# Rotation by copies, one turn for eight conditioning blocks, and tile sums added before the norm's matmul

## What is computed

```
mod_lat, mod_ctx = silu(c) @ w_ada + b_ada, silu(c_ctx) @ w_ada + b_ada     # 6144 columns each
sh_m, sc_m, gt_m, sh_f, sc_f, gt_f = split(mod_lat, 6)                      # shift, scale, gate
u = x * (1 + sc_m) + sh_m ;  u_ctx = ctx * (1 + csc_m) + csh_m
q, k, v, g, glu, gates = split(u @ w_in + b_in)
t1, t2 = split(q, 2) per head of 128 ;  rot = concat(-t2, t1)
q = q * cos + rot * sin                                                     # the same for k
o = bidirectional retention of q, k, v (8 heads), with states from u_ctx
z = depthwise convolution (31 taps) of za * sigmoid(zb)
z = silu((z - mean(z)) * rsqrt(mean((z - mean)^2) + eps) * g + b)           # over the 1024 channels
mix = (ga * (ret @ w_ret_out) + gb * (z @ w_conv_out + b_conv)) @ w_mix_out + b
h = LN(ALPHA * x + gt_m * mix) ;  mixture of 32 experts on h * (1 + sc_f) + sh_f ;  LN
```

## Time and profile before

| | us |
|---|---|
| median of 3 runs | 1581.92 |
| lowest, highest | 1580.75, 1583.12 |
| the profiled execution | 1583.5 |
| its span in the profile | 1581.6 |
| TensorE busy in the span | 1494.8 (95%) |
| VectorE busy | 492.7 (31%) |
| ScalarE busy | 214.1 (14%) |
| TensorE's mean granted clock, share of full speed | 0.986 |

### The profile page before, as it was taken

One profiled execution on the slowest core, in us unless ns is written; L12 is line 12 of the kernel. 1 busy time (PEld: TensorE's weight loads), 2 busy tenths in 40 slices (PEclk: granted clock), 3 DMA queues, 4 the chain that ended last, 5 costly groups with the idle time before them and its releaser, 6 DMA issues.

```text
span 1581.6 us, 19250 instructions
## 1 busy us (share of the span) xinstructions
PE 1494.8 (95%) x8272; PEld 948.0 (60%) x8272; DVE 492.7 (31%) x1107; ACT 214.1 (14%) x423; POOL 18.6 (1%) x39
## 2 busy tenths in 40 slices
PE   4999999999999989999999999898999899999997
PEld 2876644575588878555554444444788786555543
DVE  1546696453100125222221121123223224122222
ACT  1100100121111102311111001002022012110111
POOL 0000000000000001000000000000010000000000
PEclk8999999999999989999999999999999999999999
DMA  9522313364443464799999999999463646899996
GB/s 391 216 106 109 118 60 120 138 241 166 166 159 112 156 266 182 271 419 426 428 426 427 427 426 427 427 427 386 108 224 113 240 153 257 367 428 426 426 397 263
DMA packets 33896, 436.00 MB, mean 276 GB/s; under 512 B 4096, under 2 KB 5640, under 8 KB 7576
## 3 DMA queue, kind: packets, MB, share of 16 engines
q1 hardware_dynamic: 29520, 423.38, 66.1%
q10 hardware_dynamic: 2472, 6.41, 1.5%
q0 software_dynamic: 1824, 5.05, 0.9%
HBM read 432.19 MB, written 2.62 MB: 275 GB/s over the span
## 4 chain that ended last, share of the span: by engine, by line
PE 80%; DMA 16%; DVE 3%; ACT 1%; issue 0%; POOL 0%; SPq 0%; ACTq 0%; DVEq 0%; POOLq 0%
PE PP L751 26%; PE PP L1009 16%; PE PP L764 13%; PE PP L1024 8%; DMA RA<-in_w_moe 6%; PE MB L993 5%; DMA KQ<-in_w_moe 4%; DMA ring<-in_w_moe 4%; PE PP L985 1%; DMA ring<-in_w_glu 1%; PE PP L740 1%; PE MB L850 1%; PE MB L832 1%; DMA ring<-in_w_ada 1%; PE MB L853 1%; PE PP L1017 1%
## 5 line engine op out<-in xcount | busy, mean ns | idle before, releaser
L751 PE MATMUL PP<-uT,ring 128*128 128x256 f32 x1024 | 226.4, 384 | 3.9 <-DMA ring<-in_w_glu 3.9
L751 PEld LDWEIGHTS PP<-uT,ring 128*128 128x128 f32 x1024 | 196.8, 193 | 32.6 <-issue 5.4
L1009 PE MATMUL PP<-ring,const 128*64 128x256 f32 x1312 | 151.9, 386 | 13.2 <-DMA ring<-in_w_moe 8.0
L1009 PEld LDWEIGHTS PP<-ring,const 128*64 128x64 f32 x1312 | 96.8, 139 | 73.9 <-issue 17.1
L764 PE MATMUL PP<-ring,uT 128*128 128x512 f32 x288 | 125.1, 593 | 0.0
L1269 DVE SCALAR_TENSOR_TENSOR ZC<-ZC,vec 128x256 f32<-128x256 f32 x240 | 116.4, 485 | 8.6
L993 PE MATMUL MB<-V 64*128 64x512 f32 x400 | 112.4, 640 | 1.7 <-DVE V L1657 0.9
L1634 DVE TENSOR_SCALAR V<-V 128x1 f32<-128x1 f32 x50 | 7.7, 154 | 312.1 <-PE PP L1009 312.1
L764 PEld LDWEIGHTS PP<-ring,uT 128*128 128x128 f32 x288 | 54.4, 190 | 67.6 <-issue 67.6
L1649 DVE SCALAR_TENSOR_TENSOR V<-V 128x256 f32<-128x256 f32 x100 | 48.5, 485 | 120.5 <-PE MB L993 93.8
L764 PE MATMUL PP<-ring,RA 128*128 128x512 f32 x192 | 83.4, 592 | 0.0
(11 more groups left out here) (376 smaller groups left out, 1485.2 us busy)
## 6 DMA issues: line engine op xcount, KB each, us to landing
ring<-in_w_moe SPq DMA_DIRECT2D x61, 2048.0 KB, 18.1
RA<-in_w_moe SPq DMA_DIRECT2D x25, 2048.0 KB, 17.0
ZC<-in_w_moe SPq DMA_DIRECT2D x25, 2048.0 KB, 16.7
KQ<-in_w_moe SPq DMA_DIRECT2D x20, 2048.0 KB, 19.2
Vc<-in_w_moe SPq DMA_DIRECT2D x19, 2048.0 KB, 17.7
ring<-in_w_ada SPq DMA_DIRECT2D x12, 2048.0 KB, 8.4
ring<-in_w_gates SPq DMA_DIRECT2D x7, 2048.0 KB, 7.9
ring<-in_w_v SPq DMA_DIRECT2D x5, 2048.0 KB, 7.7
```

The costliest lines, as they stand in the source:

```text
L751: ins = pe.matmul(out[:, c, :], W[:, k * width + at:k * width + at + P], X[:, k, :], start=k == 0, stop=k == K - 1)
L1009: ins = pe.matmul(bank[q][SLOTS * g:SLOTS * (g + 1), 0:L], x[:, k, :], W[:, k * 512 + g * 256:k * 512 + (g + 1) * 256], start=k == 0, stop ...
```

## The change

Rotation: `rotate`, its matrix and its eight matmuls go. After `raw_copy`, ScalarE copies partitions 64 to 127 of `raw` to 0 to 63 of a buffer `swapped` (the memory of `Ph`), and 0 to 63 to 64 to 127; the sign goes into the sine table. The PSUM pair is released before these copies.

Conditioning: for blocks 4 to 11, the window of `sT` that serves as the left side is moved by one column per block, so that block 4 + i puts its result into row i of each group of 32 and zero into the others. All eight accumulate in one PSUM pair, which is copied once and turned once with an eight-column selection. The later jobs' pairs are counted anew. `late_modulation` follows the statistics of the last head.

Norm: VectorE adds the eight tiles of `conv` (behind the last convolution step), and later of the squares (behind `ret(0)`), into `rs`; one matmul for each sum remains.

```diff
-                     ("rot", 128), ("pick", 2), ...
+                     ("pick", 9), ...
-                    dense += 1
+                    dense += src != "ada" or b < 4 or b == 11
-        sT = sb("sT", [P, DT, 32])
+        sT = sb("sT", [P, DT, 40])
+        swapped = Ph
-            nc.scalar.activation(sT[:, :, 0:2], cin[:, :, :], ACT.Silu).then_inc(silu_c, 1)
+            nc.scalar.activation(sT[:, :, 0:9:8], cin[:, :, :], ACT.Silu).then_inc(silu_c, 1)
...
-                ins.then_inc(pair_free[j["pair"]], 1)
+                say(act, ins, pair_free[j["pair"]], j["use"] + 1)
+                nc.scalar.activation(swapped[0:64], raw[64:128], ACT.Copy)
+                nc.scalar.activation(swapped[64:128], raw[0:64], ACT.Copy).then_inc(raw_swapped, 1)
...
-                        ins = pe.matmul(out[at:at + 32, 0:2, :]..., sT[:, k, :],
-                                        W[:, k * 512:(k + 1) * 512], start=k < 4, stop=k >= 4, tile_position=(0, at))
+                        at, late = 32 * (k % 4), j["b"] - 4
+                        x = sT[:, k, 0:32] if late < 0 else sT[:, k, 8 - late:40 - late]
+                        ins = pe.matmul(out[at:at + 32, 0:2, :]..., x, W[:, k * 512:(k + 1) * 512],
+                                        start=k < 4 and late <= 0, stop=k >= 4 and late in (-4, -3, -2, -1, 7), ...)
...
+            def turn_late():
+                pe.wait_ge(ada_kept, 5)
+                for c in range(4):
+                    ins = pe.matmul(PP[J["ada", 11, 0]["pair"]][:, 2, 8 * c:8 * c + 8], adaR[:, 0, c * P:(c + 1) * P],
+                                    cst("pick", 8), start=True, stop=True)
+                ins.then_inc(ada_turned, 1)
...
-            def rotate(r): ...            # and its four calls
...
                 job(J["ada", 4 + h, 0])
                 mix_head(h)
-                turn_ada(4 + h)
+            turn_late()
...
-            def mean_sums(): ...          # eight matmuls
-            def square_sums(): ...        # eight matmuls
+            def mean_of_sums(ready, out, done):
+                ln_wait(pe, ready, 1)
+                pe.matmul(out[:, 0, :], ones, rs[:, :], start=True, stop=True).then_inc(LN[done], 1)
             pe.wait_ge(ret_kept, 4)
-            mean_sums()
+            mean_of_sums("in", MB[0], "mean")
             job(J["ret", 0, 0])
             job(J["ret", 1, 0])
-            square_sums()
+            mean_of_sums("squares", MB[1], "summed")
...
+            def late_modulation():
+                dve.wait_ge(ada_turned, 5)
+                ...                       # one addition for all eight blocks, then the nine operations of b == 11 before
...
+                        link(ins)
+                        ln_say(dve, V_.tensor_reduce(rs[:, :], conv.rearrange("p k n -> p n k"), AX.X, ALU.add), "in", 1)
...
                 V_.tensor_tensor(Eqd[:, :, :], raw[:, :, :], cos4, ALU.mult)
-                for q in range(2):
-                    ins = V_.tensor_tensor(dst[:, 2 * q:2 * q + 2, :], MB[q][:, :, :], sin2, ALU.mult)
-                link(ins)
+                link(V_.tensor_tensor(dst, swapped[:, :, :], sin4, ALU.mult))
...
-                keep_ada(4 + h)
                 if h:
-                    modulation(3 + h)
                     stats(h - 1)
                 if h + 2 < HEADS:
                     decay_q(h + 2)
-            modulation(11)
+            job_wait(dve, J["ada", 11, 0])
+            say(dve, V_.tensor_copy(adaR[:, 0, :], PPt[J["ada", 11, 0]["pair"]][:, 0, :]), ada_kept, 5)
             stats(HEADS - 1)
+            late_modulation()
...
+            def add_squares():
+                ln_wait(dve, "squared", 2)
+                V_.tensor_reduce(rs[:, :], SQ.rearrange("p k n -> p n k"), AX.X, ALU.add).then_inc(LN["squares"], 1)
...
             centre()
             ret(0)
+            add_squares()
             ret(1)
             divide()
...
-    put("sin", np.sin(ang).T)
+    put("sin", np.sin(ang).T * np.where(p < 64, -1.0, 1.0)[:, None])
```

More of the change, by code:

```diff
@@ L217, in build @@
         MB = [ctx.enter_context(nc.psum_tensor(f"MB{i}", [P, 2, L], F32)) for i in range(4)]
-        bank = [flat(PP[i // 2])[:, 512 * (i % 2):512 * (i % 2 + 1)] for i in range(4)]
+        held = J["mix", 0, 0]["pair"]
+        assert held == J["out2", 0, 0]["pair"]
+        bank = [flat(PP[(held + i // 2) % 2])[:, 512 * (i % 2):512 * (i % 2 + 1)] for i in range(4)]
         spread = (bank[3], flat(MB[2]))
@@ L275, in build @@
         mix_in, h_scaled = sem("mix_in"), sem("h_scaled")
-        LN = {k: sem(f"ln_{k}") for k in ("in", "mean", "centred", "squared", "summed", "rooted", "divided", "out_a", "out_v")}
+        LN = {k: sem(f"ln_{k}") for k in ("in", "mean", "centred", "squared", "squares", "summed", "rooted", "divided", "out_a", "out_v")}
         def ln_wait(eng, step, value):
@@ L738, in job @@
                     for k in range(DT):
-                        at = 32 * (k % 4)
-                        ins = pe.matmul(out[at:at + 32, 0:2, :].rearrange("p a n -> p (a n)"), sT[:, k, :],
-                                        W[:, k * 512:(k + 1) * 512], start=k < 4, stop=k >= 4, tile_position=(0, at))
+                        at, late = 32 * (k % 4), j["b"] - 4
+                        x = sT[:, k, 0:32] if late < 0 else sT[:, k, 8 - late:40 - late]
+                        ins = pe.matmul(out[at:at + 32, 0:2, :].rearrange("p a n -> p (a n)"), x, W[:, k * 512:(k + 1) * 512],
+                                        start=k < 4 and late <= 0, stop=k >= 4 and late in (-4, -3, -2, -1, 7), tile_position=(0, at))
                 elif kind in ("cm8", "cm4", "cm16"):
@@ L781, in turn_ada @@
                     ins = pe.matmul(PP[J["ada", b, 0]["pair"]][:, 2, 2 * c:2 * c + 2], adaR[:, b % 2, c * P:(c + 1) * P],
-                                    cst("pick", 2), start=True, stop=True)
+                                    cst("pick", 9)[:, 0:9:8], start=True, stop=True)
+                ins.then_inc(ada_turned, 1)
+            def turn_late():
+                pe.wait_ge(ada_kept, 5)
+                for c in range(4):
+                    ins = pe.matmul(PP[J["ada", 11, 0]["pair"]][:, 2, 8 * c:8 * c + 8], adaR[:, 0, c * P:(c + 1) * P], cst("pick", 8),
+                                    start=True, stop=True)
                 ins.then_inc(ada_turned, 1)
@@ L795, in _ @@
                 job(J["glu", b, 0])
[L797 to L801, removed]
-                for q in range(2):
-                    ins = pe.matmul(MB[q][:, :, :].rearrange("p a n -> p (a n)"), rotm,
-                                    raw[:, 2 * q:2 * q + 2, :].rearrange("p a n -> p (a n)"), start=True, stop=True)
-                ins.then_inc(raw_rot, 1)
             for b in range(2):
@@ L1845, in constants @@
     put("ones", np.full((P, P), 1.0 / D))
[L1846 to L1849, removed]
     pos = np.arange(L)
@@ L1896, in layout @@
     d["xT"], d["ctxT"] = tiles(i["x"][0]), tiles(i["ctx"][0])
-    d["cT"] = np.concatenate([tiles(i["c"]), tiles(i["c_ctx"][None])], axis=2)
+    d["cT"] = np.concatenate([tiles(i["c_ctx"][None]), tiles(i["c"])], axis=2)
     for n, (x, y, z) in enumerate((("w_exp_gate", "w_exp_up", "w_exp_down"), ("expert_w_gate_2", "expert_w_up_2", "expert_w_down_2"))):
```

60 lines of the change are left out of this document (22 added, 38 removed).

## The result

The changed kernel takes 1560.39 us (median of 4 runs, 1557.5 to 1561.82) against 1582.03 for the kernel before beside it: ratio 0.986, 95% interval 0.9845 to 0.9876. The direction held, and so did the reasons for the work that was removed. The time lies 3.2 us under the forecast of 1563.6 and 0.1 us under the lower end of its range, 1560.5: 21.6 us were gained where 18.3 were forecast. Two later comparisons of the same kernel give ratios of 0.9854 (0.9838 to 0.987) and 0.9842 (0.9826 to 0.9858), and the forecast of 1563.6 against 1581.92 is a ratio of 0.9884, above the upper end of all three intervals. The gain was too small in the forecast, and not by chance.

What follows compares the result with a forecast made beforehand. The prediction took TensorE's nearly unbroken chain as the bound: 6.88 + 5.67 + 6.04 = 18.59 us, less 0.4, plus 0.15, is 18.3 us off, so 1563.6 us from a median of 1581.92; range 1560.5 to 1569.0.

Steps and rivals of the forecast that it cites:

- What bounds the kernel: First glu to last cout job: TensorE runs without a break except 1.2 us, so removed matmuls there shorten the span.
- Rotation: k, q and v jobs: removing four pieces of 1.72 us saves 6.88 us; ScalarE's swap copies replacing them cost 0.
- The walk through VectorE's queue: First v block: `with_bias` starts at 195.5, and its margin before TensorE wants the pair grows from 2.6 to 8 us.
- Rival B: k, q and v jobs: slow copies across partitions lose the rotation's 6.88 us, giving 1570.5 us; chance 0.05.
- Conditioning: Loop over heads: eight turns become one, saving 5.67 us, less 0.4 us for a 0.07 us wait in six heads.
- Rival A: Head loop: VectorE sets the pace, 0.6 to 4.9 us come back, giving 1564 to 1568.5 us; chance 0.14.
- Norm: Norm's two sums: removed matmuls save 6.04 us; two VectorE reductions of 3.6 us each are hidden at cost 0.
- Start: First 37 us, paced by loads: early constants shrink by 62 KB, saving 0.15 us.
- Does it reach the end: Experts' stage: its first loads start earlier by as much as the jobs end earlier, and the later stages move whole.
- rival C: Experts' stage: full DMA engines swallow the gain, so the time stays at 1581.9 us; chance 0.04.
- rival D: Experts' stage: weights from shifted `const` buffers slow each of 46 experts; at 0.5 us each, 1587 us; chance 0.03.
- The sum: Whole kernel: 18.59 us off TensorE's chain, less 0.4, plus 0.15, makes a gain of 18.3 us.

Runs made afterwards that it cites:

- rot_only: The kernel before with only the rotation's part of the change, the unused matrix kept in the constants: 1575.41 us, ratio 0.9959.
- norm_only: The kernel before with only the norm's part of the change: 1576.95 us, ratio 0.9965.
- pad_before_cout: The changed kernel with 43 unread matmuls, 36.9 us of TensorE, ahead of the first cout job: 1598.75 us, ratio 1.0096.
- after_shift32, 64 and 128: The changed kernel with 32, 64 or 128 unused bytes a partition behind the constants: 1560.77, 1562.34 and 1562.32 us.
- before_again: The kernel before, unedited, traced a second time: 1580.98 us, ratio 0.9992.
- before_shift32: The kernel before with 32 unused bytes a partition between the constants and the next buffer: 1579.44 us, ratio 0.9983.

## Why the prediction missed its range

Two steps failed. The rate of the loads in the experts' stage was put down as unchanged, and its term at nothing; it was worth 2.4 us in the changed kernel. And the term of the conditioning was mis-sized, 5.3 us where 6.14 were measured. Together they are the 3.2 us by which the forecast missed. The lower end of the range was missed by only 0.1 us, but the two later comparisons miss it by more.

**What bounds the kernel**: right. All three objects lay end to end in TensorE's queue, and their removal shows one for one.

**Rotation**: 6.88 forecast, 6.87 measured in rot_only (185.67 less 178.80 us) and 6.80 in the changed kernel. The 0.07 us go with the norm's part, whose first reduction stands in the same stretch: norm_only has 185.74 there. The swap takes 2 x 1.06 us as taken from the earlier trace rows. The walk through VectorE's queue gave `with_bias` at 195.5; it starts at 193.95, and ends at 195.17, 10.5 us before TensorE writes the pair again (205.71), where 2.6 us had been. Rival B is out.

**Conditioning**: the mis-sized term. Forecast 5.67 - 0.4 = 5.3, measured 6.14 in every trace with it. Two things were wrong. A wait does exist, but it is the weight load's and does not reach the matmuls: VectorE ends the weighting at 301.46 + 0.68 = 302.14, and the load of L839 follows 0.06 us later, where I had taken 0.12 from one row. In the next head VectorE ends at 309.62 + 0.68 = 310.30, and the load starts 0.05 us later, 0.11 us behind the end of the load before it, where the kernel before leaves 0.03 (307.51 + 1.60 to 309.14):

```profile
300.44 1.70 PEld L833 LDWEIGHTS MB<-Vc,small 128*128 128x128 f32 x8
302.20 0.80 PEld L839 LDWEIGHTS MB<-KQ 128*128 128x128 f32 x4
...
308.54 1.70 PEld L833 LDWEIGHTS MB<-Vc,small 128*128 128x128 f32 x8
310.35 0.75 PEld L839 LDWEIGHTS MB<-KQ 128*128 128x128 f32 x4
```

The matmuls start at 302.38 and 310.48 without a gap, 1.73 us behind those of L833 in both heads. And the turn cost more than its own 0.81 us. As I read the rows, its weight loads, back to back, also delayed the weight load of the next group. In the kernel before, the group of L832 starts its matmuls 0.03 us behind its first weight load and lasts 1.81 us:

```profile
306.52 1.08 PEld L781 LDWEIGHTS PP<-const,small 128*128 128x128 f32 x8
307.51 1.60 PEld L832 LDWEIGHTS MB<-Vc,small 128*128 128x128 f32 x8
```

In the changed kernel the load leads by 0.21 us (300.44 to 300.65) and the group lasts 1.73. So a removed turn is worth 0.89 us with a group of scores behind it. Six of the seven have one: 6 x 0.89 + 0.81 = 6.15 us, against 6.14 measured. Rival A, the only one to which I gave more than 0.05, is out. (Its upper end was also summed wrongly: 4.9 in place of 0.4 us gives 1568.1, not 1568.5.)

**Norm**: 6.04 forecast, 6.05 measured; the strided reduction at 3.67 us against 3.6. The estimate from the strided row and its 1.68 ns an element was the right one. The fixed 0.15 us is not in the contiguous row shown; it comes out with a second one of the same line, 2286 ns for 2048 elements.

**Start**: 0.15 us of gain forecast. The first glu job starts at 37.77, 37.73 and 38.67 us in three traces of the changed kernel and at 37.39 and 38.24 in two of before. The spread hides it.

**Does it reach the end**: this step failed. That the stages behind move as a whole is right (pad_before_cout; rival C is out). But I took the rate of the loads as given, 427 GB/s, though from 848 us on the chain of the kernel before goes through DMA for 192 of the 249 us left of that stage, and looked at the moved addresses only as weights of TensorE (rival D, which is out: the groups with weights from `const` have the same mean, 380 ns, in the kernel before and in the changed one):

```profile
L1009 PE MATMUL PP<-KQ,const 128*64 128x256 f32 x448 | 51.0, 380 | 2.9 <-DMA KQ<-in_w_moe 2.7
L999 PE MATMUL PP<-KQ,const 128*64 128x256 f32 x448 | 51.0, 380 | 2.6 <-DMA KQ<-in_w_moe 2.5
```

The bays had moved too. Four of them came to lie at a multiple of 256 bytes, the loads ran at 430 GB/s, and the stage became shorter: 470.1 us in the mean of after_shift32, 64 and 128, against 467.7 in the mean of three traces of the changed kernel, 2.4 us. In the kernel before, the same step was 3.2 us: 471.02 in before_again against 467.79 in before_shift32, both without the half-clock group. A page of the Trainium skill bears on it (DMA: Bandwidth & Descriptors, How a descriptor splits into AXI transactions): when a descriptor does not start at a multiple of 256 bytes, its first transaction starts at the boundary below, and the bytes ahead of the start are fetched without use. The trace agrees with the unit, by the shifts of 32, 64, 128 and 256 bytes. That page of the Trainium skill tells it of reads, and what was moved here is the side that is written, so that the reason is not shown. By its rule I estimate 4096 x 4 = 16384 bytes in 65 instead of 64 transactions, 1.6% for each moved bay and 0.9% for four of seven; measured are 0.7% for four (149.37 to 150.48 MB), and nothing for the other three.

**The sum**: 6.80 + 6.14 + 6.05 + 2.4 = 21.4 us, against 21.6 in the first comparison. The 23.1 and 24.6 us of the two later ones leave 1.7 and 3.2 us without a shown cause, or 0.9 and 2.4 if the 3.2 us of the kernel before are taken in place of 2.4. Between the two first traces the spans differ by 23.6 us: 19.0 in the three terms, 0.6 up to the first gather, 4.3 in the first experts' stage and 0.4 behind it, less 0.7 of a later start. One candidate is seen but not shown: the first gate matrix of the first expert, behind 2.34 us of idle time, takes 5.3 us in place of 3.7, with the granted clock at 0.72 in the 6 us around it, so that part of them went at the lower of its two levels:

```profile
649.31 5.26 PE L1009 MATMUL PP<-ring,const 128*64 128x256 f32 x32 [2.34 <-ACT const L620]
```
```profile
648.00:654.00 6.00, 4.69 (x30) 2.79 (x32) 0.00 (x0) 1.15 (x3) 0.00 (x0) 0.72 0.61 262
```

and the same in the changed kernel, at full clock:

```profile
630.49 3.67 PE L999 MATMUL PP<-ring,const 128*64 128x256 f32 x32 [2.34 <-ACT const L625]
```
```profile
629.00:635.00 6.00, 4.51 (x34) 2.70 (x35) 0.00 (x0) 1.71 (x4) 0.00 (x0) 1.00 0.64 273
```

The slow form stands in four of the six traces without the full change and in none of the twelve with it. No run was made to find what decides it. The two traces of the kernel before, one with it and one without, differ by 1.0 us in the first experts' stage. The range was too narrow for another reason also: it reached 3.1 us below the forecast of 1563.6 and 5.4 above it, and every named rival was one that made the kernel slower.

## What to carry to other kernels

Where a removed instruction lies end to end on the engine that bounds, count its issue time from the rows and take it as it is; here three such terms repeated to 0.1 us over 18 traces. Where a later stage is paced by loads, its rate is a term of the sum: ask whether the change moves any buffer that the loads write, and look at the start addresses before and after. Name a rival on the side of the gain as well, and give it room in the range.

## What was not expected of the hardware

- Bays that begin at a multiple of 256 bytes in the partition were loaded faster, in rows of 16 KB: 149.4 MB in 350 us with none of seven so placed, 149.9 with two, 150.3 with three, 150.5 with four or more. 32 bytes of padding were worth 0.17% of the kernel before (0.9983, 0.9972 to 0.9995).
- ScalarE's copy from partitions 64 to 127 into 0 to 63 took 1.06 us for 1024 elements, the same as a pass over 1024 elements on all 128 partitions.
- A group of matmuls with two columns cost the group behind it 0.08 us more than its own 0.81 us (1.81 us with it, 1.73 without); that this goes through the order of the weight loads is my reading of their rows.
